# A hybrid decoder trunk: the recurrent branch's last preparation runs in one piece, its bonus sum comes at the tenth fill, and ScalarE's work before a norm is reordered

## The reference

```
x += 0.5 * SwiGLU_a(rms(x))
h = rms(x); P = h @ w_in
A = retention(P[ret]);  B = Mamba-2 SSD(P[ssm]);  C = RWKV-7(P[rwkv])
x += w_out( sum_i sigmoid(P[gate_i]) * (branch_i @ w_branch_i) )
x += CrossAttn(rms(x), memory)
x += 0.5 * SwiGLU_b(rms(x))
```

```
mixed = cols + (prev - cols) * mu            r, kc, vc, wd, ad, gd = split(mixed)
decay, a_lr, g_rw = functions of (wd, ad, gd) by small products
kk = normalised(kc * k_k);  kc = kc * (1 + (a_lr - 1) * k_a)
bonus = sum_head(r * kc * r_k) * vc
then the scan over tokens with r, decay, kc, vc, kk, kk * a_lr
```

## Time and profile before

| | us |
|---|---|
| median of 3 runs (3106.17 to 3111.55) | 3109.57 |
| profiled execution, its own time | 3115.79 |
| its span | 3114.1 |
| PE busy, share of the span | 2844.1, 91% |
| DVE, ACT, POOL busy | 1755.5, 1253.0, 521.4 |

### The profile page before, as it was taken

One profiled execution on the slowest core, in us unless ns is written; L12 is line 12 of the kernel. 1 busy time (PEld: TensorE's weight loads), 2 busy tenths in 40 slices (PEclk: granted clock), 3 DMA queues, 4 the chain that ended last, 5 costly groups with the idle time before them and its releaser, 6 DMA issues. The chain is left out here.

```text
span 3114.1 us, 63966 instructions
## 1 busy us (share of the span) xinstructions
PE 2844.1 (91%) x25694; PEld 2645.1 (85%) x25694; DVE 1755.5 (56%) x2645; ACT 1253.0 (40%) x1739; POOL 521.4 (17%) x341
## 2 busy tenths in 40 slices
PE   7998989989988999899999988989898899998997
PEld 7998888777787898799889978987787788887997
DVE  4444764586576565544354458445756766655443
ACT  4534522254323443444254355222542234434542
POOL 0003650054400000000000046401543000000000
PEclk9999999999998999899999999999999989998998
DMA  4444340135374466344344443401454554663443
GB/s 164 148 148 140 118 141 18 37 115 181 109 278 162 158 211 220 129 149 148 116 152 148 149 134 112 126 24 34 138 176 144 224 213 128 221 222 119 149 148 105
DMA packets 119694, 448.21 MB, mean 144 GB/s; under 512 B 13648, under 2 KB 23920, under 8 KB 111664
## 3 DMA queue, kind: packets, MB, share of 16 engines
q1 hardware_dynamic: 97920, 329.78, 32.9%
q0 software_dynamic: 21552, 115.34, 10.1%
HBM read 397.04 MB, written 48.02 MB: 143 GB/s over the span
## 5 line engine op out<-in xcount | busy, mean ns | idle before, releaser
L1532 ACT ACTIVATE w_high<-ring 128x1024 fp32r<-128x1024 f32 x598 | 631.8, 1057 | 761.1 <-PE gemm_banks L902 320.9
L898 PE MATMUL gemm_banks<-in_high,w_high 128*128 128x320 f32 (+1 forms) x2720 | 802.3, 311 | 26.9 <-ACT w_high L1532 14.7
L1936 DVE TENSOR_TENSOR w_low<-ring,w_high 128x1024 fp32r<-128x1024 f32 x436 | 532.7, 1222 | 477.4 <-ACT w_high L1532 476.7
L899 PE MATMUL gemm_banks<-in_low,w_high 128*128 128x320 f32 (+1 forms) x2720 | 794.7, 308 | 0.0
L733 POOL TENSOR_TENSOR w_low<-ring,w_high 128x1024 fp32r<-128x1024 f32 x162 | 414.0, 2564 | 968.1 <-ACT w_high L1532 966.6
L898 PEld LDWEIGHTS gemm_banks<-in_high,w_high 128*128 128x128 f32 x2720 | 514.3, 189 | 33.8 <-issue 14.7
L899 PEld LDWEIGHTS gemm_banks<-in_low,w_high 128*128 128x128 f32 x2720 | 514.1, 189 | 1.7
L902 PE MATMUL gemm_banks<-in_high,w_low 128*128 128x320 f32 (+1 forms) x2720 | 451.0, 308 | 6.9 <-POOL w_low L733 3.9
L902 PEld LDWEIGHTS gemm_banks<-in_high,w_low 128*128 128x128 f32 x2720 | 408.8, 189 | 9.9 <-POOL w_low L733 5.1
L947 PE MATMUL gemm_banks<-in_high,w_high 128*128 128x320 f32 x640 | 209.2, 339 | 21.8 <-DVE arena L2062 16.7
L974 PE MATMUL gemm_banks<-act_high,w_high 128*128 128x320 f32 x704 | 208.3, 309 | 2.6 <-DVE arena L1985 2.6
(11 more groups left out here) (414 smaller groups left out, 4229.4 us busy)
## 6 DMA issues: line engine op xcount, KB each, us to landing
ring<-in_w SPq DMA_DIRECT2D x598, 512.0 KB, 3.6
arena<-in_kc POOLq DMA_DIRECT2D x14, 1024.0 KB, 6.6
arena<-in_vc POOLq DMA_DIRECT2D x14, 1024.0 KB, 7.3
out_fill<-stage SPq DMA_DIRECT2D x80, 160.0 KB, 4.0
arena<-in_ssm POOLq DMA_DIRECT2D x16, 512.0 KB, 13.6
out_s_ssm<-arena POOLq DMA_DIRECT2D x16, 512.0 KB, 14.0
arena<-in_ret POOLq DMA_DIRECT2D x16, 512.0 KB, 22.2
out_s_ret<-arena POOLq DMA_DIRECT2D x16, 512.0 KB, 7.1
```

What stands on the lines that cost most here:

```text
L898: mm(dst, w_high[:, slot, w(k)], in_high[:, k, 0:n], start=(k == 0), stop=False)
L899: mm(dst, w_high[:, slot, w(k)], in_low[:, k, 0:n], start=False, stop=False)
L1532: f(w_high[:, slot], ring[:, s, 0:D], ACT.Copy).then_inc(weights_high, 1)
L1936: tt(w_low[:, slot], ring[:, pos % RING, 0:D], w_high[:, slot].bitcast(F32), ALU.subtract).then_inc(weights_split, 1)
```

## The change

VectorE: what stood at c = 22 to 25 goes into a new function `finish_rwkv`, called once after all 26 evacuations. Four large products in it are cut into two halves of four channel groups each. TensorE: the bonus sum comes after ten fills instead of four, with five behind it instead of eleven. ScalarE: only the high part of the first RWKV chunk is made before the last square; that of the second chunk follows after the high parts of h. The table load of `norm` stays only for `ffb`; one is put ahead of the layer loop and one at the start of each second FFN, after the last gate. GpSimd's program is not edited.

```diff
+RKS_AFTER = 10
...
             def rwkv():                                     # TensorE
-                fill("fill_rwkv", 4)
+                fill("fill_rwkv", RKS_AFTER)
                 need(pre_v, "rk")
                 need(pre_v, "mixed")
                 tile_sums(pre_p, "rks", K("bones"), E3)
-                fill("fill_rwkv", PREP_FILLS - 4)
+                fill("fill_rwkv", PREP_FILLS - RKS_AFTER)
                 need(pre_v, "done")
...
             def norm(tag):                                  # ScalarE
-                nc.scalar.preload_act_table_set("natural_log_exp_and_others")
+                if tag == "ffb":
+                    nc.scalar.preload_act_table_set("natural_log_exp_and_others")
...
                 act_.wait_ge(gated, g0 + FT)
+                nc.scalar.preload_act_table_set("natural_log_exp_and_others")
...
                             if i == KT - 1 and seg == "ffa13":
-                                first_weights("rwkv")
+                                weights(0, RING, BASE["rwkv"])
                             square(second, nsq, i, ...)
...
+            nc.scalar.preload_act_table_set("natural_log_exp_and_others")
             act_.wait_ge(x_here, 32)
...
                 high_parts("mix", h, n_full)
+                weights(0, RING, BASE["rwkv"] + 1)
                 rwkv_columns()
...
                     prepare_rwkv(c)                         # VectorE
                 dve.wait_ge(psum_free, RING + b + RT + 2)
+                finish_rwkv()
...
+            def finish_rwkv():
+                (b0, b1), (r0_, r1_), (v0, v1) = sum_spans(), spans(rr), spans(vv)
+                for i in range(KT):
+                    ins_ = stt(E3[:, i], rr[:, i], PR("r_k", i), kk_[:, i], ALU.mult, ALU.mult)
+                    V_(ins_) if i < KT - 1 else V_.mark(ins_, pre_v, "rk")
+                ...
+                for a in (0, 4):
+                    V_(tt(ar0[:, a:a + 4, :, 1:C64], kkc[:, a:a + 4, :, 1:C64], ec[:, a:a + 4, :, 0:C64 - 1], ALU.mult))
+                ...
+                for a in (0, 4):
+                    V_(tt(kk_[:, a:a + 4], kk_[:, a:a + 4], LW[:, a:a + 4], ALU.mult))
+                V_(tt(Bt[:, 0:4], Bt[:, 0:4], Aa[:, 0:4], ALU.mult))
+                V_.mark(tt(Bt[:, 4:8], Bt[:, 4:8], Aa[:, 4:8], ALU.mult), pre_v, "mixed")
+                need(pre_p, "rks")
+                V_(tt(r0_, b0, v0, ALU.mult))
+                V_.mark(tt(r1_, b1, v1, ALU.mult), pre_v, "bonus")
```

More of the change, by code:

```diff
@@ L2088, in prepare_rwkv @@
             def prepare_rwkv(c):
-                (b0, b1), (r0_, r1_), (v0, v1) = sum_spans(), spans(rr), spans(vv)
                 if c in (16, 18):
@@ L2106, in prepare_rwkv @@
                     V_(tt(Bt, Bt, E3, ALU.mult))
[L2107 to L2129, removed]
+            def finish_rwkv():
[3 more added lines that the diff above has]
+                    V_(ins_) if i < KT - 1 else V_.mark(ins_, pre_v, "rk")
+                ar0, kkc, ec = AR[:, :, 0:NCH, 0], chunks64(Bt[:, :, 0:TP]), chunks64(E[:, :, 0:TP])
+                for a in (0, 4):
+                    V_(tt(ar0[:, a:a + 4, :, 1:C64], kkc[:, a:a + 4, :, 1:C64], ec[:, a:a + 4, :, 0:C64 - 1], ALU.mult))
+                V_(copy(ar0[:, :, :, 0], kkc[:, :, :, 0]))
+                V_(copy(pend, ec[:, :, :, C64 - 1]))
+                ar0 = AR[:, :, NCH, 0].rearrange("p a (b t) -> p a b t", t=SL)
+                kkc, ec = (v[:, :, TP:T].rearrange("p a (b t) -> p a b t", t=SL) for v in (Bt, E))
+                V_(tt(ar0[:, :, :, 1:SL], kkc[:, :, :, 1:SL], ec[:, :, :, 0:SL - 1], ALU.mult))
+                V_(copy(ar0[:, :, :, 0], kkc[:, :, :, 0]))
+                V_(copy(pends, ec[:, :, :, SL - 1]))
+                for a in (0, 4):
[5 more added lines that the diff above has]
+                V_.mark(tt(r1_, b1, v1, ALU.mult), pre_v, "bonus")
+                arrived(dve, layer, "x_stored")
+                arrived(dve, layer, "shift_stored")
```

## The result

The changed kernel takes 3129.44 us (median of 10 runs, 3126.09 to 3140.05). The kernel before, run beside it, takes 3113.34 us (median of 10, 3106.17 to 3128.78). The ratio is 1.0045, with a 95% interval of 1.0029 to 1.006: 14 us slower (9 to 19); the medians themselves are 16 us apart. The forecast was +10 and 3119, with a range up to 3126. So the direction came out as forecast, and the time lies above the range. Of the 20 us between 3109.57 and 3129.44 some 4 belong to the kernel before, which stood at 3113.34 here. The profiled execution has a span of 3127.9 us against 3114.1, and its mean granted clock is 0.956.

A forecast was written before the change was run, and what follows sets the result against it. TensorE, busy 91% of the span, was taken as the bound, with waits ended by VectorE's evacuations. +18.0 (two layers behind the columns) − 5.4 (norm) − 2.6 (table loads) = +10.0 on 3109.6, about 3119 us; range 3105 to 3126.

The forecast's parts named there:

- Parts 1 to 3: Behind the RWKV columns: they end at 386.5, not 401.8; `mixed` comes at 409.5; TensorE stands 10 us at fill 4.
- Part 2: VectorE's moved products: 14.4 us of their own plus 8.5 us of GpSimd splits that exclude them, so `mixed` at 409.5.
- Part 4: Bonus sum to scan: VectorE's work covered by five fills, not eleven; scan starts 8.6 us later; +9.0 a layer, +18.0.
- Part 5: Norm before the mixer, last square first: `Ln` 4.0 us earlier, 1.3 lost again; net 2.7 a layer, −5.4 in two.
- Part 6: Table loads: both bare loads at the program's end go, −2.6 us; the moved ones cost nothing.
- rival C: Loads at the end stay and one of 1.28 us comes before `Exp` in layer one: +3.9, 3123; chance 0.07.
- A: Rival: VectorE and GpSimd share time better, `mixed` at 401 to 404, kernel faster, 3102 to 3107; chance 0.14.
- B: Rival: `mixed` near 406 to 408, or small products fit between splits; 4 to 6 a layer, 3110 to 3114; chance 0.22.
- D: Rival at the norm: last part of h not held by the split, full 4.0 gain, 3117; 0.57 together with the forecast.

The follow-up runs named there:

- e12: Changed kernel with GpSimd's splits of fills 0 to 3 cut to 64 of 1024 elements: 3115.29 us, ratio 0.9986 to the kernel before.
- e10: Changed kernel with the four large products whole, not in halves: 3136.60 us, ratio 1.005 to the kernel before.
- e2: Kernel before with the VectorE and TensorE edits alone: 3130.69 us, ratio 1.0029 to the kernel before.
- e3: Changed kernel with the bonus sum back behind fill 4: 3121.41 us, ratio 0.9999 to the kernel before.
- e4: Changed kernel with GpSimd's wait for `mixed` and the shift store moved behind the split of fill 9: 3104.27 us, ratio 0.9941 to the kernel before.
- e5: Kernel before with the three table-load edits alone: 3114.29 us, ratio 0.9992 to the kernel before.
- e1: Kernel before with all of ScalarE's edits alone: 3122.32 us, ratio 1.0007 to the kernel before.
- e13: Kernel before with only GpSimd's LoRA load and store of x issued later, behind the third chunk's split: 3122.39 us, ratio 1.0021.
- e14: The same kernel as e4, run once more: 3109.94 us, ratio 0.9974 to the kernel before.
- e6: Kernel before with ScalarE's edits, GpSimd issuing the LoRA load and store of x before the second chunk's split and memset: 3108.84 us, ratio 0.9976.

## Why the forecast had the direction and not the size

**Parts 1 to 3, right.** The moved products start without idle after the last evacuation. Part 2 reckoned 14.4 us of products and 8.5 of splits; e12 has 15.0 without splits, and the splits add 7.7. Fill 4 stands 9.99 us for 10 forecast. (By the prediction's own terms fill 3 ends at 400.2 and not at 400.6; nothing hangs on it.) That the halves buy nothing here is shown by e10.

**Part 4, right in mechanism, too dear.** It put +9.0 on a layer, 18.0 in all; the trace has +7.5 and +7.9, 15.4. The scan starts without idle as forecast. In layer one the 1.4 us lie in three places. From the columns to the low matmuls of fill 4 it took 29.7 us, as forecast: the splits added 0.8 less than part 2 said, and the products took 0.6 more. From there to the first of VectorE's sixteen small products it took 0.5 us less, and from that one to the end of `memset(Ys)` 20.9 for 21.5 (the rows before give 21.2). The last 0.4 were for the scan itself. It runs at a granted clock of 0.50 from 465 to 475 us, as part 4 feared, and still takes 17.5 us from its first product to ScalarE's first instruction behind chunk 0 (line 1734), as before; the low clock cost nothing there. The ratio of e2 says less than the trace: e2, which has parts 1 to 4 alone, is 9 us slower (4 to 14), and 18 lies outside that. e3 (14 us back) and e4 confirm the cause: too few fills behind the bonus sum, with GpSimd's wait at the fourth fill in front of it.

**Part 5, the step that failed.** Its gain was right: −2.7 a layer forecast, −2.8 to −3.0 in every kernel where the transfers go out in time. The failed sentence is that on the LoRA load: "TensorE needs the load only behind chunk 3 ... so I cost this at nothing, and 1 us a layer if that cover fails." I asked who waits for the LoRA load, and nobody did. I did not ask what its 1.0 MB and the 1.28 MB of x would do to the ring loads beside which they now lie, nor what stands in ScalarE's queue behind a copy that waits for such a load. The cost was 4.1 us a layer over fourteen layers, 8 in all, and in the profiled execution 7.3 (+1.9 for the −5.4 forecast). It turned a gain of 5.4 us into a small loss: +10 plus these 7.3 less the 2.6 of part 4 is the +14.7 of the balance. GpSimd's queue was listed in part 5 as going back "by some 3 us against TensorE"; it went back 6.7 (9.5 us after the first matmul for 2.8), since the second split and the `memset` both stood ahead of the transfers and the first matmul came 4.3 earlier.

**Part 6, right.** Both loads went, at 2.6 us in the trace of the changed kernel and of e5. The Trainium skill, "ScalarE activation tables: per-element evaluation and per-set limits", section "Table sets in the compiler and the runtime", has loads placed per block; in these traces the table loaded inside the layer loop still stood behind it, so the measurement decides, and rival C falls with it.

**Luck.** That +10 lies within 4 us of the 14 is in part luck. By the ratios of e1 and e2, parts 5 and 6 came out at +2 where −8 was forecast, and parts 1 to 4 at +9 where +18 was forecast: each half missed by 9 to 10 us, in opposite directions.

**The rivals.** A needed `mixed` near 404, and it came at 412.04. B's split schedule did not occur: VectorE never waited for TensorE before the scan. D (the last part of h not held) is refuted: the four low parts took 5.45 us for 3.40, a split of 2.81 lying in them, as part 5 said.

**What stays open.** What e13 loses beyond the 4 us that its stages show; when the copy of 32 elements takes 0.2 and when 2.3 us, which moves kernels with the old preparation by some 2 us a layer; why e2's ratio shows 9 us where its trace shows 15; and why the same kernel gave 0.9941 as e4 and 0.9974 as e14.

## What to carry to other kernels

When an engine's step is moved, price each transfer it issues by what it will lie beside, not only by who waits for it: 2.3 MB issued 6.7 us later against the columns cost 4 us a layer, though no engine waited for these transfers themselves. An engine that waits for a late load also holds back what stands behind it in its queue; here that was what TensorE stood for. When work is gathered behind a mark, look for every engine that waits for that mark in order; here the bonus sum moved to the tenth fill and one wait on GpSimd stayed at the fourth, and moving it turned 14 us of loss into a gain of 8 to 18. For VectorE products out of SBUF and GpSimd splits, adding both up as one queue came close here (7.7 us added of 9.3).

## What the runs showed of the hardware

- TensorE's stands of 0.74 us (e13), 0.87 (e12, layer one), 1.86 (changed kernel, layer two) and 1.88 us (e4, layer two) behind the norm were followed by 6 us at a granted clock of 1.00, that of 2.67 us (changed kernel, layer one) by 6 us at 0.50.
- The exclusion holds for the small products with three operands as well: eight of 0.55 us took 4.77 us beside the tiny splits of e12 and 12.43 beside 9.3 us of full splits, while each split lost only 0.0 to 0.3 us.
- Between 268 and 296 us, loads of 512 KB landed in 3.9 us (median of five) with the 2.3 MB on the other queue issued at 271.49, and in 6.4 us with them issued at 273.90; the longest took 11.3 us. The 2.3 MB in turn took 13.2 and 9.3 us for 9.7 and 6.7. In e6, with them issued at 267.00, the loads landed in 3.5 us (median of six).
